# A decoder step with 32 experts: the slots of an expert's tokens are turned by two from expert to expert, and the code of the end moves into the branch

## The reference

```python
    lc = (xt @ w_router_c).astype(F32) + b_router_c.astype(F32)
    pc = jax.nn.softmax(lc, axis=-1)
    grp = jnp.argmax(lc, axis=-1)
    ...
    topv, topi = lax.top_k(pf, TOP_K)
    wts = gate_c * topv / jnp.sum(topv, axis=-1, keepdims=True)
    eid = grp[:, None] * EXPERTS_PER_GROUP + topi
    ...
    def expert_block(args):
        xblk, e = args
        hid = jax.nn.silu(xblk @ w_gate[e]) * (xblk @ w_up[e])
        return hid @ w_down[e]
    ...
    y_prompt = rmsnorm(xp, final_norm_g)
    y_sample = rmsnorm(xs, final_norm_g)
```

## Time and profile before

| | us |
|---|---|
| median of 3 runs | 1956.11 (1955.09 to 1959.73) |
| profiled execution | 1960.08 |
| its span, first to last instruction | 1958.3 |
| TensorE matmul busy | 1812.6 (93%) |
| VectorE busy | 688.0 (35%) |
| ScalarE busy | 481.7 (25%) |
| GpSimd busy | 112.3 (6%) |
| mean granted TensorE clock | 0.974 |
| DMA moved | 545.99 MB, mean 279 GB/s |

### The profile page before, as it was taken

The page is one execution under the profiler, slowest core; times in us unless marked ns, Lnnn a source line. Parts: engine busy times, 40 slices in busy tenths (PEclk is TensorE's granted clock), DMA queues, the critical chain, the costliest instruction groups (busy, mean ns, idle before and its releaser), DMA issues.

```text
span 1958.3 us, 35913 instructions
## 1 busy us (share of the span) xinstructions
PE 1812.6 (93%) x15607; PEld 1242.8 (63%) x15607; DVE 688.0 (35%) x1296; ACT 481.7 (25%) x836; POOL 112.3 (6%) x115
## 2 busy tenths in 40 slices
PE   6999997997989999898999999999999999999994
PEld 5999997875666799686455554444554444554541
DVE  4437776545566543754411111111111111111113
ACT  4446653341222422732311111011000000000001
POOL 0000002300101000000000000000000000000000
PEclk7999999898999999999999999999999999999998
DMA  7644540214535673548899999999999999999995
GB/s 220 158 131 123 145 122 4 67 30 130 162 117 209 190 218 84 172 120 320 310 374 429 421 423 427 423 396 406 421 423 426 421 420 397 413 422 427 422 425 201
DMA packets 191392, 545.99 MB, mean 279 GB/s; under 512 B 39227, under 2 KB 146844, under 8 KB 163566
## 3 DMA queue, kind: packets, MB, share of 16 engines
q1 hardware_dynamic: 184080, 518.03, 69.3%
q0 software_dynamic: 6768, 26.09, 4.3%
q10 hardware_dynamic: 438, 0.32, 0.1%
HBM read 524.86 MB, written 28.06 MB: 282 GB/s over the span
## 4 chain that ended last, share of the span: by engine, by line
DMA 28%; PE 21%; DVE 1%; issue 1%; SPq 0%; DVEq 0%
DMA w_expert<-in_w_up_dram 27%; PE p_u L2951 8%; PE p_y L2967 4%; PE p_g L2951 4%; PE p_xg L2919 3%; DMA w_expert<-in_w_down_dram 1%; PE p_xgT L2934 1%; PE p_g L2926 0%; DVE w_expert L3112 0%; DVE w_expert L3121 0%; PE p_xgT L2940 0%; PE p_xgT L3026 0%; PE p_y L2974 0%; PE p_xg L3026 0%; DVE y_slots L3067 0%
## 5 line engine op out<-in xcount | busy, mean ns | idle before, releaser
L2951 PE MATMUL p_u<-w_expert,xgT 128*64 128x256 f32 x2048 | 239.6, 388 | 34.0 <-DMA w_expert<-in_w_up_dram 33.9
L2951 PE MATMUL p_g<-w_expert,xgT 128*64 128x256 f32 x2048 | 232.0, 379 | 0.9 <-DVE xgT L3051 0.9
L2951 PEld LDWEIGHTS p_u<-w_expert,xgT 128*64 128x64 f32 x2048 | 148.4, 140 | 117.8 <-DMA w_expert<-in_w_up_dram 43.5
L2967 PE MATMUL p_y<-w_expert,hidT 128*64 128x512 f32 x960 | 217.8, 595 | 0.8 <-DVE hidT L3063 0.5
L2951 PEld LDWEIGHTS p_g<-w_expert,xgT 128*64 128x64 f32 x2048 | 147.1, 137 | 87.5 <-issue 18.4
L2919 PE MATMUL p_xg<-low,slot_sel 128*64 128x512 f32 x768 | 177.9, 598 | 0.0
L2967 PEld LDWEIGHTS p_y<-w_expert,hidT 128*64 128x64 f32 x960 | 66.2, 137 | 126.0 <-issue 124.1
L3056 DVE CAST row<-rowf 128x1 int32<-128x1 f32 x32 | 4.9, 153 | 355.9 <-POOLq L3193 355.9
L3141 ACT ACTIVATE act_g<-p_g 128x256 f32<-128x256 f32 x32 | 12.3, 384 | 449.5 <-PE p_u L2951 449.5
L2919 PEld LDWEIGHTS p_xg<-low,slot_sel 128*64 128x64 f32 x768 | 52.5, 137 | 80.7 <-issue 74.2
L426 PE MATMUL in_acc<-x_high,w_in_high 128*128 128x320 f32 (+2 forms) x560 | 93.9, 320 | 8.2 <-ACT w_in_high L458 8.2
(11 more groups left out here) (601 smaller groups left out, 2480.9 us busy)
## 6 DMA issues: line engine op xcount, KB each, us to landing
w_expert<-in_w_gate_dram SPq DMA_DIRECT2D x64, 2048.0 KB, 21.7
w_expert<-in_w_up_dram SPq DMA_DIRECT2D x64, 2048.0 KB, 23.3
w_expert<-in_w_down_dram SPq DMA_DIRECT2D x60, 2048.0 KB, 20.5
w_in_raw<-in_w_in_dram SPq DMA_DIRECT2D x32, 1024.0 KB, 5.8
ho_raw<-in_w_out_dram SPq DMA_DIRECT2D x12, 1024.0 KB, 6.5
q_lat<-in_w_out_dram SPq DMA_DIRECT2D x4, 1024.0 KB, 8.3
mem_k_s<-in_cache_mem_k_dram SPq DMA_DIRECT2D x8, 512.0 KB, 7.0
mem_v_s<-in_cache_mem_v_dram SPq DMA_DIRECT2D x8, 512.0 KB, 11.9
```

The costliest lines, as they stand in the source:

```text
L2951: mm = pe.matmul(acc[SL * h:SL * h + SL, 0:FF // 2], xgT[:, t, g // 2, :], w[g][:, FF * t + FF // 2 * h:FF * t + FF // 2 * h + FF // 2], s ...
L2967: mm = pe.matmul(p_y[SL * h:SL * h + SL, 512 * b:512 * b + 512], hidT[:, j, g, :], tile, start=(g == 0 and j == 0), stop=(g == 1 and j == 1))
```

## The change

Two things, and nothing else.

The slots are turned. `slot_of` is 192 wide, 1 to 64 three times, and `select` of expert k looks at 128 of them from column 2k on. The token of rank j of expert k then stands in column (j - 1 - 2k) mod 64 of each half, so its rows of `y` stand on other partitions. Everything behind it (`gather`, `find_rows`, `selT`) goes by `sel` and follows. `rearrange` and `bass.ds(k, SL)` only express the start 2k by the loop's counter.

The end is written twice. `rounds` takes it as a function. If the largest count is below 65, the engine goes on into the end right behind `body(0)`; the further rounds, with an end of their own, stand on the other side. This is done on all five engines; only SyncE's and TensorE's are shown, those of VectorE, ScalarE and GpSimd are moved in the same way.

```diff
@@ memory_out_and_route, GpSimd
-                step(pool.iota(S.slot_of[:, :], pattern=[[0, 2], [1, SL]], base=1, channel_multiplier=0,
+                step(pool.iota(S.slot_of[:, :], pattern=[[0, 3], [1, SL]], base=1, channel_multiplier=0,
                                allow_small_or_imprecise_dtypes=True))
@@ experts
-        def rounds(eng, body):
+        def rounds(eng, body, end):
 
             most = body(0)
-            with eng.If(most > SL):
+            with eng.If(most < SL + 1):
+                end()
+            with eng.Else():
                 with eng.Fori(1, SLOTS_MAX // SL) as r:
                     body(r)
+                end()
             eng.nop()
@@ SyncE
-                rounds(sp, body)
-                sp.wait_ge(y_kept, 1)
-                for i, n in enumerate(TILE):
-                    sp.dma_start(S.final_x[i][0:n, :], S.x2_dram[128 * i:128 * i + n, :]).then_inc(S.final_in[i], 16)
...
+                def end():
+                    sp.wait_ge(y_kept, 1)
+                    for i, n in enumerate(TILE):
+                        sp.dma_start(S.final_x[i][0:n, :], S.x2_dram[128 * i:128 * i + n, :]).then_inc(S.final_in[i], 16)
+                    sp.dma_start(S.final_g, d['final_norm_g'].unsqueeze(0).to_broadcast([128, D])).then_inc(S.final_g_in, 16)
+                    for i, n in enumerate(TILE):
+                        sp.wait_ge(ready, i + 1)
+                        dst = outs[0][0, 128 * i:128 * i + 128, :] if i < 2 else outs[1].rearrange("b t n -> (b t) n")
+                        sp.dma_start(dst, out[i][0:n, :]).then_inc(stored, 16)
+                    sp.wait_ge(stored, 48)
+
+                rounds(sp, body, end)
@@ TensorE
-                rounds(pe, body)
-                for i, n in enumerate(TILE):
...
+                def end():
+                    for i, n in enumerate(TILE):
+                        for b in range(2):
+                            if i == 2:
+                                pe.wait_ge(last_added, 2 + 2 * b)
+                            for h in range(2):
+                                hh = slice(SL * h, SL * h + SL)
+                                pe.matmul(into[i][2 * b + h][0:n, :], selT[hh, i, 0:n], y[hh, 512 * b:512 * b + 512], start=True, stop=True).then_inc(scattered, 1)
+
+                rounds(pe, body, end)
@@ VectorE, select
+                    slots = S.slot_of[:, :].rearrange("p (q s) -> p q s", s=2)[:, bass.ds(k, SL), :].rearrange("p q s -> p (q s)")
                     for i in range(3):
-                        ins = dve.tensor_scalar(sel[:, i, :], S.slot_of[:, :], slot_shift, S.pos_of[:, i, bass.ds(k, 1)], ALU.add, ALU.is_equal)
+                        ins = dve.tensor_scalar(sel[:, i, :], slots, slot_shift, S.pos_of[:, i, bass.ds(k, 1)], ALU.add, ALU.is_equal)
                     ins.then_inc(sel_made, 1)
@@ build
-        S.slot_of = sb("slot_of", [128, 2 * SL]); S.no_row = sb("no_row", [128, 1]); S.row_base = sb("row_base", [128, 1]); S.row_of = sb("row_of", [128, 3, NE, 4])
+        S.slot_of = sb("slot_of", [128, 3 * SL]); S.no_row = sb("no_row", [128, 1]); S.row_base = sb("row_base", [128, 1]); S.row_of = sb("row_of", [128, 3, NE, 4])
```

More of the change, by code:

```diff
@@ L2902, in _ @@
                 load_still(sp, d, S, 3, 1)
-                rounds(sp, body)
-                sp.wait_ge(y_kept, 1)
-                for i, n in enumerate(TILE):
-                    sp.dma_start(S.final_x[i][0:n, :], S.x2_dram[128 * i:128 * i + n, :]).then_inc(S.final_in[i], 16)
-                sp.dma_start(S.final_g, d['final_norm_g'].unsqueeze(0).to_broadcast([128, D])).then_inc(S.final_g_in, 16)
-                for i, n in enumerate(TILE):
[L2909 to L2912, removed]
+                def end():
[9 more added lines that the diff above has]
+                rounds(sp, body, end)
             @block.tensor
@@ L3101, in body @@
                     return most
-                rounds(dve, body)
                 def add_last(i):
@@ L3121, in scale, with end @@
                     dve.scalar_tensor_tensor(out[i][0:n, :], x[i][0:n, :], ss[0:n, i, 2:3], S.final_g[0:n, :], ALU.mult, ALU.mult).then_inc(ready, 1)
[L3123 to L3128, removed]
+                def end():
+                    add_last(0)
+                    add_last(1)
+                    scale(0)
+                    add_last(2)
+                    scale(1)
+                    scale(2)
+                rounds(dve, body, end)
             @block.scalar
@@ L3168, in body, with end @@
                     return most
[L3169 to L3176, removed]
+                def end():
+                    for i, n in enumerate(TILE):
+                        act.wait_ge(last_added, 4 * i + 4)
+                        if i:
+                            act.wait_ge(squared, i)
+                        act.activation(squares[0:n, :], x[i][0:n, :], ACT.Square, accum_out=ss[0:n, i, 0:1]).then_inc(squared, 1)
+                        act.wait_ge(squared, i + 1)
+                        act.activation(ss[0:n, i, 1:2], ss[0:n, i, 0:1], ACT.Sqrt, bias=S.eps[0:n, :], scale=1.0 / D).then_inc(root, 1)
+                rounds(act, body, end)
             @block.gpsimd
@@ L3203, in body, with end @@
                     return most
-                rounds(pool, body)
-                pool.nop().then_inc(y_kept, 1)
+                def end():
+                    pool.nop().then_inc(y_kept, 1)
+                rounds(pool, body, end)
 def build(nc, d, outs):
```

## The result

The changed kernel takes 1947.16 us in the median of 6 runs (1941.33 to 1948.16), the kernel before 1957.92 beside it; the ratio is 0.9939, with a 95% interval of 0.9924 to 0.9954. Measured again with the experiments, on a chip where the kernel before took 1959.33, the ratio was 0.9911 (0.9889 to 0.9932). The forecast of -14.8 us on 1956.1 is a ratio of 0.9924, between the two: the medians are 10.8 us apart in the first measurement, and the ratio of the second makes 17.4 us. The profiled execution took 1942.4 us. Two executions beside the experiments, one of 3683 us (the kernel before) and one of 4392 us (turn by four + end), were slow and are in no ratio.

The account below looks back on a forecast made before the run. The expert stage was taken as bound by TensorE after a still and otherwise by unevenly loaded DMA engines. -8.1 - 6.9 + 0.1 + 0.1 = -14.8 us took the median 1956.11 to 1941.3 us, range 1934.5 to 1951.5.

Parts of the forecast that it names:

- -8.1 for the turn: Expert stage: turning the slots evens scatter rows over DMA engines, saving 8.1 us, with ends 2.6 and 15.3.
- -6.9 for the end: End of the kernel: without TensorE's 7488 ns jump, the first scale starts when final_norm_g lands, saving 6.9 us.
- +0.2 for what is added: Added cost: 0.1 us for the longer select and iota, 0.1 us for SyncE's jump at the very end.
- sign to look for: In the profile after, scale(0) starts 16 to 17 us after the issue of final_norm_g, not 23.
- The end 7.5: Upper bound of the gain at the end: TensorE's whole jump, 7.5 us, if final_norm_g comes earlier too.
- TensorE's wait stays: Rival at the branch: the one-round side isn't loaded either, so TensorE still waits; 1948.2 us, chance 0.07.
- SyncE pays: Rival at the very end: SyncE's last jump costs what TensorE's did, +7.5 us; 1948.7 us, chance 0.05.
- The price of a row: Expert-stage scatters: a 4 KB row costs a DMA engine 0.33 us, from readings of 0.32 and 0.35.
- upper end of 15.3 us: Turn's largest gain: 40.9 us of rows on an engine with four in every scatter, against a mean of 25.7.
- 7.2 us off the full balance: Taken from the turn's 15.3 us: idle time of leading engines at both stills, 4.0 and 3.2 us, thought unavoidable.
- the lower end: Turn's least gain, 2.6 us: the slow turn leaves a stretch's worst engine 40 rows, not 44, saving 1.3 us twice.
- The slow engines: Rival in the expert stage: engines without rows are slow for weights, and the turn loads them; 1965.2 us, chance 0.06.

Follow-up runs that it names:

- turn by four + end: The changed kernel with the slots turned by four an expert instead of two; ratio 0.9910 to the kernel before, stage 899.98 us.
- end alone: Kernel before plus only the end placed behind the branch, slots not turned; ratio 0.9953, 9.2 us faster, stage 910.69 us.
- balanced kernels: Kernels with ranks distributed evenly over the DMA engines and the new end; against the kernel before, ratio 0.9906 without a turn, 0.9884 turned by four.
- packed kernel: Kernel before with slots reordered to put as many ranks as possible on one DMA engine, no turn; ratio 1.0236, 46 us slower.
- spread turned by four: Kernel before with ranks balanced over engines, slots turned by four an expert, and the new end; ratio 0.9884, or 0.9873 with final_norm_g loaded third.
- turn alone: Kernel before plus only the slots turned by two an expert, old end kept; ratio 0.9952, 9.4 us faster, stage 906.20 us.
- spread: Kernel before with a fixed slot order balancing each scatter over the DMA engines, no turn, old end; ratio 0.9941, 11.5 us faster, stage 898.67 us.

## Why the prediction was right, and where it wasn't

Forecast were -8.1 for the turn, -6.9 for the end and +0.2 for what is added. The pieces of the two profiles of the changed kernel are -8.9 and -4.5 (stage), -8.5 twice (y copy to scale) and +0.4 (scale to end). Both parts work by the mechanism that was forecast; the turn gave less than forecast in the mean, the end more.

**The end.** Forecast -6.9 for the branch, with final_norm_g as the next late thing, and +0.1 for SyncE's last jump. Measured: from the y copy to the scale -8.5 in the changed kernel (twice) and -7.2 with the end alone. The mechanism was right, and so was what comes next: in the end alone and in the balanced kernels VectorE waits for final_norm_g. The mis-sized term is its landing. I took 16.5 us from its issue, and 16 to 17 as the sign to look for; in the changed kernel it was 14.7 and 14.8, and the bound became VectorE's adds, 7.3 us behind the y copy; elsewhere it was 15.9 to 17.8. The end 7.5 that I gave as the upper bound was too low, since the first matmuls also ran slower behind the jump (below). SyncE's jump cost 0.3 to 0.4 us, not 0.1: the branch row itself is 38 ns, and what follows it comes later. TensorE's 7.5 was no guide. The rivals "TensorE's wait stays" and "SyncE pays" are out.

**The price of a row.** 0.33 us taken, 0.32 to 0.35 read, 0.37 from the packed kernel. The map of slots to engines, read from two bursts, holds; the bursts alone gave only four neighbouring slots to an engine, and the packed kernel added the four 32 further. The upper end of 15.3 us for a full balance was right: 16.0 and 14.4 us measured with the spread turned by four.

**The turn.** Forecast -8.1; the stage is 8.9, 4.5 and 4.5 us shorter, 6.0 in the mean, and the timed runs with the turn alone give 9.4 with an interval of 6 to 13, which may hold some of the shorter jump. The number is in place within that spread, but one step behind it failed. I took 7.2 us off the full balance because at the stills the mean engine would wait for buffers anyway. It doesn't: with the spread turned by four, the DMA share over both stills is 1.01, and the stage is shorter by the whole 15.3 (16.0 and 14.4). The idle engines at the stills were a result of the imbalance and not a second bound. What really holds the turn by two back is the other step, which I had named and then used only for the lower end: twenty slots that move by two lie over one engine for ten experts. The balance of each scatter by itself (spread, 12.1 us) and the quicker turn (one profile, 10.8) both get more. Counted by the map from the rows of the 31 scatters (22 to 58 each), the engine with most carries 124 rows before, 85 with the turn by two, and 91 with the spread or the turn by four, so the total doesn't explain the order. The 11 experts between the stills do: there the engine with most has 44 rows before, 42 with the turn by two, 33 with the spread and 34 with the turn by four (the mean is 28). The turn by two fell 9 us short of the balanced stage (6.0 for 15.2 in the mean) and I had taken off 7.2 for another reason. That the two met at about the same size is luck.

**What is added.** The select has one register operation more, 40 ns for the 57 forecast, before a wait of 355.6 us; the iota went from 251 to 309 ns. Neither shows.

**The slow engines,** the rival on the other side, are out: the spread and both turns load the engines more evenly, those without rows among them, and are faster.

**The spread of the runs.** 1955 to 1961 before and 1941 to 1948 after, with the part before the first scatter moving by up to 16 us between profiles. Where that comes from was not looked into. Nor is it settled what makes the stage with the same turn by two take 901.8 in one profile and 906.2 in two, while three profiles without it agree to 0.4 us. What the timelines show is where: at the 31st scatter the three are 11.4, 8.0 and 6.7 us ahead of the kernel before, and 2.0 us of the first one's lead over the other two arise between the 22nd and the 23rd, behind the second still, where its DMA share stays at 1.00 and theirs falls. Behind the 31st scatter all three lose 2.3 to 3.6 us again; in all three the last 32 p_u matmuls take 5.36 us in place of 3.67, after a wait of 2.4 to 3.1 us.

## What to carry to other kernels

When a stage is bound by DMA and TensorE waits though the mean DMA share is near full, ask whether all 16 engines are: compare the share just before a late landing, and count how many packets of a scatter start at once. If an indirect DMA fills only the first partitions, put its rows on every fourth partition first; here one line of index pattern was worth at least as much as the turn and added no instruction. Code that follows a long skipped body was reached here by a far jump; put the path that is taken right behind the branch, and look for what lands next. Add a wait to the busy time of the matmuls behind it before you compare two profiles, since a wait can lower the clock and come back as slower matmuls.

## What the runs showed of the hardware

A far jump of TensorE took 3.7 us with idle DMA engines and up to 8.2 us in the shadow of the 3.7 MB of last loads, by the wait of one instruction packet; going on behind the branch took 0.08 us, loop branches about 0.2 (208 ns in the median of 20).

On the kernel before, the pause of the jump costs once more behind it. Stretches of the kernel before, then one of the changed kernel; the third column from the end is the granted clock:

```profile
1929.00:1936.00 7.00, 0.00 (x0) 0.00 (x0) 0.00 (x0) 0.00 (x0) 0.00 (x0) 0.78 0.62 162
1936.00:1939.00 3.00, 2.31 (x6) 1.19 (x8) 0.13 (x1) 0.00 (x0) 0.00 (x0) 0.50 0.03 11
```

```profile
1919.00:1923.00 4.00, 3.38 (x16) 1.52 (x16) 2.49 (x5) 0.23 (x1) 0.00 (x0) 1.00 0.72 233
```

TensorE had done nothing for 7 us, and the granted clock fell to 0.50, the 1.2 GHz level, for the first matmuls: the first four took 2.08 us in place of 1.13. Without the pause it stayed at 1.00, 2.4 GHz.

An accumulating scatter cost the most loaded DMA engine some 0.33 to 0.37 us a 4 KB row, and by the packed kernel and the spread, which engine that is follows from the partition.
